# A two-block network on one core: the norms of the second block tile by tile, shifted copies on two engines, and the entries of the feed-forward stages reordered

## The chip, the core and the metric

The kernel runs on one core of one Trainium2 chip, as a single program of its five engines: TensorE (PE), VectorE (DVE), ScalarE (ACT), GpSimd (POOL) and SyncE (SP), which here issues all the DMAs. The metric is the time of the whole program on the device in microseconds (us). The profile's span runs from the first to the last instruction; the program's time is a little longer.

## The reference

Two blocks follow one another on a batch of one, 256 tokens (two tiles of 128), width 1024, all in float32.

```
h = x
for l in 0, 1:                                   # first block
    h = layer_norm(a*h + 0.5*swiglu(h, ffn1[l]))     # hidden width 2816
    h = layer_norm(a*h + mixer(h))                   # three branches: delta rule, conv, latent attention
    h = layer_norm(a*h + 0.5*swiglu(h, ffn2[l]))
# second block: four residual steps j = 0..3, each
#   shift, scale, gate = split(silu(c) @ mod_w[j] + mod_b[j])
#   x = x + gate * fn_j(rms_norm(x, g[j]) * (1 + scale) + shift)
# fn_0: short convolution (in 1024 -> 3072, 3 taps, out)   fn_1: swiglu
# fn_2: dilated attention                                 fn_3: router, top 2 of 8 experts, swiglu each
out = rms_norm(x, final_g)
```

## The kernel before, in words

Everything stays in SBUF: H holds the 256 rows as two tiles t = 0, 1 of [128, 1024]. Each engine has a program of its own in which the stages stand in a fixed, hand-written order; semaphores join them. There is no planner. Weights come by SP in tiles of 1 MB.

**Split products.** In the first block and in the FFNs each float32 operand is split into a high part (ScalarE's copy into the rounded format, semaphores ..._high) and a remainder (VectorE's subtraction, L1058 for weights, ..._low), and each product is three matmuls (L715, L716, L717).

**An FFN** (ffn_pe, ffn_act, ffn_vec) has NS = 11 steps of 256 hidden columns. TensorE does gate(0), up(0), gate(1), up(1), down(0), then in a loop gate(s), up(s), down(s-1), and last down for tile 0 and then for tile 1, so that the norm of tile 0 starts early. VectorE's step s is: remainder of gate(s+1); one part of the modulation (mod_vec, L1048 and L1051: eight operations that add mod_w rows into mod_sum, in four of the five FFNs); unit product silu(gate)*up; remainders of up(s+1) and down(s); remainder of the unit. Before it stands the split of the stage's input: turned_act (L935) and turned_vec (L1079) in the first block, x_high_act and x_low_vec (L1073) in the second. SP asks for the next weights when the remainder of the last ones is done (gate_load, up_load, down_load), in program order with mod_load.

**Norms of the first block.** layer_norm on VectorE: L1178 adds the residual (one operand in PSUM), L1181 and L1183 take the statistics, L1186 and L1190 subtract, scale and shift (two operands in SBUF each); std_act on ScalarE (L1028) takes the root between them. Then TensorE turns the tile (turn_h, L711). After the second FFN of a layer TensorE first sums mod_sum by mod_pe (L889: 24 blocks, two matmul records each), which ScalarE takes to mod_col (mod_act). spin (L883) is matmuls whose result is not used.

**Norms of the second block**, for j = 0..3: residual on VectorE (L2395, L2397) with the gate's row, rms_act on ScalarE (square L2246, root L2248, both tiles in turn), norm_vec (L2383) on VectorE, turns on TensorE (norm_pe), then norm_act: ScalarE makes eight scaled and shifted copies of 256 columns to HT (L2256), two for each of four PSUM banks ("quarters"), and after them two copies of the gate's row (L2265), which TensorE has made by four matmul records (L2075) from diag. TensorE waits for HT (ht_ready) and for the row (grow_ready) before it goes on to the stage: L2095 (convolution in), the FFN, L2127 (attention projections) or L2192 (router).

GpSimd has only the constants, one product per layer (L688) and five products per layer of 128x1024 (L695) in the mixer.

## Time and profile before

| what | value |
|---|---|
| time, median of 3 runs | 3021.76 us (3019.57 to 3026.18) |
| the profiled execution's own time | 3022.93 us |
| its span | 3021.2 us |
| mean granted clock of TensorE | 0.981 |
| TensorE busy | 2888.2 us, 96% |
| VectorE busy | 2016.1 us, 67% |
| ScalarE busy | 1440.2 us, 48% |
| GpSimd busy | 52.8 us, 2% |
| memory read | 657.23 MB, 218 GB/s over the span |
| chain that ended last | PE 76%, DVE 9%, PEld 4%, issue 3%, ACT 3% |
| one operation of L1051, mean | 484 ns |

The chain that ended last is followed back from the last instruction to whatever released each one. A granted clock of 1 is 2.4 GHz, 0.5 is 1.2 GHz. In a row of the timeline the first two numbers are start and duration in us, "x8" is the number of instructions merged in the row, and the square brackets tell how long the engine idled before it and whose instruction ended that. In a table of windows the busy time of PE, PEld, DVE, ACT and POOL follows the length.

### The profile page before, as it was taken

How to read it: one execution, taken by the hardware profiler on the slowest of the kernel's cores; microseconds unless marked ns; L12 is line 12 of the kernel's file. 1: busy time of each engine (PE TensorE's matmuls, PEld its weight loads, DVE VectorE, ACT ScalarE, POOL GpSimd, SP SyncE). 2: the span in 40 equal slices, each digit the busy share in tenths (PEclk: the TensorE clock that was granted, in tenths of full speed). 3: DMA queues.
4: the chain of work that ended last, by engine and by line, in shares of the span. 5: the costliest groups of instructions: out<-in, count | busy, mean ns of one | idle time of the engine just before them, and what ended most of it. 6: DMA issues, size and time to landing. Idle time of an engine off the chain costs nothing.

```text
span 3021.2 us, 43641 instructions
## 1 busy us (share of the span) xinstructions
PE 2888.2 (96%) x16718; PEld 2451.4 (81%) x16718; DVE 2016.1 (67%) x2457; ACT 1440.2 (48%) x1600; POOL 52.8 (2%) x93
## 2 busy tenths in 40 slices
PE   8999898999999998899999999988999999999997
PEld 8998886699899988758988699455888888888886
DVE  6767963477777787327651444154898889888987
ACT  4434621244444462114530344133777777777775
POOL 2000010000000001000000000000000000000000
PEclk9999999999999999999999999998999999999999
DMA  8755512486777442137743455323999999999995
GB/s 296 249 168 174 158 57 86 147 270 222 243 246 237 154 139 96 58 112 259 242 139 140 151 186 179 106 74 121 358 349 339 349 348 347 341 349 348 347 341 210
DMA packets 398878, 659.74 MB, mean 218 GB/s; under 512 B 14090, under 2 KB 241272, under 8 KB 398776
## 3 DMA queue, kind: packets, MB, share of 16 engines
q1 hardware_dynamic: 398776, 658.32, 63.1%
q8 instruction: 72, 1.18, 0.2%
q14 instruction: 30, 0.25, 0.0%
HBM read 657.23 MB, written 1.05 MB: 218 GB/s over the span
## 4 chain that ended last, share of the span: by engine, by line
PE 76%; DVE 9%; PEld 4%; issue 3%; ACT 3%; DVEq 2%; DMA 1%; PEldq 1%; ACTq 0%; SPq 0%
PE banks L715 20%; PE banks L716 19%; PE banks L717 19%; PE banks L2095 3%; PE banks L2127 3%; PE banks L1392 2%; PE banks L711 2%; DVE ffn_arena L1058 1%; PE banks L788 1%; DVE mod_sum L1051 1%; PE banks L889 1%; PEld banks L1392 1%; PE banks L883 1%; DVE panel_rest L1744 1%; PE banks L1362 1%
## 5 line engine op out<-in xcount | busy, mean ns | idle before, releaser
L715 PE MATMUL banks<-ffn_arena 128*128 128x256 f32 (+1 forms) x3460 | 1163.3, 336 | 23.3 <-DVE ffn_arena L1079 10.3
L717 PE MATMUL banks<-ffn_arena 128*128 128x256 f32 (+1 forms) x3460 | 1148.6, 332 | 0.0
L715 PEld LDWEIGHTS banks<-ffn_arena 128*128 128x128 f32 x3460 | 660.4, 191 | 93.8 <-DVE ffn_arena L1079 12.6
L717 PEld LDWEIGHTS banks<-ffn_arena 128*128 128x128 f32 x3460 | 660.3, 191 | 69.5
L1120 DVE TENSOR_TENSOR expert_rest<-expert_raw,ffn_arena 128x2048 fp32r<-128x2048 f32 (+1 forms) x306 | 646.8, 2159 | 83.9 <-ACT ffn_arena L977 79.4
L716 PE MATMUL banks<-ffn_arena 128*128 128x256 f32 (+1 forms) x2200 | 672.2, 306 | 0.0
L977 ACT ACTIVATE ffn_arena<-expert_raw 128x2048 fp32r<-128x2048 f32 (+1 forms) x306 | 539.4, 1815 | 66.9 <-PE banks L717 64.5
L716 PE MATMUL banks<-expert_rest,ffn_arena 128*128 128x512 f32 (+1 forms) x1224 | 465.8, 381 | 0.0
L716 PEld LDWEIGHTS banks<-ffn_arena 128*128 128x128 f32 x2200 | 422.9, 192 | 17.4 <-issue 0.5
L716 PEld LDWEIGHTS banks<-expert_rest,ffn_arena 128*128 128x128 f32 x1224 | 230.0, 188 | 42.8
L1058 DVE TENSOR_TENSOR ffn_arena<-gate_w,ffn_arena 128x1024 fp32r<-128x1024 f32 x110 | 130.0, 1223 | 195.5 <-ACT ffn_arena L912 195.5
L912 ACT ACTIVATE ffn_arena<-down_w 128x1024 fp32r<-128x1024 f32 x110 | 110.4, 1051 | 162.1 <-PE banks L717 149.4
L715 PE MATMUL banks<-ffn_arena,mix_high 128*128 128x256 f32 x640 | 181.9, 284 | 4.6 <-DVE panel_rest L1744 2.6
L717 PE MATMUL banks<-ffn_arena,panel_rest 128*128 128x256 f32 x640 | 180.0, 281 | 0.0
L716 PE MATMUL banks<-ffn_arena,mix_high 128*128 128x256 f32 x640 | 180.0, 281 | 0.0
L1051 DVE SCALAR_TENSOR_TENSOR mod_sum<-mod_unit,misc_col,mod_sum 128x256 f32 (+1 forms) x336 | 162.7, 484 | 25.1
L912 ACT ACTIVATE ffn_arena<-up_w 128x1024 fp32r<-128x1024 f32 x110 | 110.5, 1053 | 120.4 <-PE banks L717 111.6
L1058 DVE TENSOR_TENSOR ffn_arena<-down_w,ffn_arena 128x1024 fp32r<-128x1024 f32 x110 | 129.6, 1219 | 48.5 <-ACT ffn_arena L912 48.5
L912 ACT ACTIVATE ffn_arena<-gate_w 128x1024 fp32r<-128x1024 f32 x110 | 109.9, 1050 | 65.4 <-PEq L2110 59.9
L1542 ACT ACTIVATE arena<-banks 128x512 f32<-128x512 f32 (+3 forms) x100 | 55.2, 592 | 175.4 <-PE banks L1352 52.5
L1058 DVE TENSOR_TENSOR ffn_arena<-up_w,ffn_arena 128x1024 fp32r<-128x1024 f32 x110 | 129.6, 1219 | 4.7 <-ACT ffn_arena L912 4.7
L1744 DVE TENSOR_TENSOR panel_rest<-panel,mix_high 128x2048 fp32r<-128x2048 f32 x48 | 109.6, 2286 | 30.6 <-ACT mix_high L1542 30.2
(412 smaller groups left out, 3410.3 us busy)
## 6 DMA issues: line engine op xcount, KB each, us to landing
expert_raw<-in_moe_w_gate_dram SPq DMA_DIRECT2D x90, 1024.0 KB, 5.3
expert_raw<-in_moe_w_up_dram SPq DMA_DIRECT2D x90, 1024.0 KB, 5.4
expert_raw<-in_moe_w_down_dram SPq DMA_DIRECT2D x90, 1024.0 KB, 5.1
gate_w<-in_ffn_w_gate_dram SPq DMA_DIRECT2D x55, 1024.0 KB, 5.3
up_w<-in_ffn_w_up_dram SPq DMA_DIRECT2D x55, 1024.0 KB, 5.4
down_w<-in_ffn_w_down_dram SPq DMA_DIRECT2D x55, 1024.0 KB, 5.4
mod_unit<-in_mod_w_dram SPq DMA_DIRECT2D x48, 1024.0 KB, 5.2
panel<-in_w_in_dram SPq DMA_DIRECT2D x48, 1024.0 KB, 5.4
```

Of the source, the lines that this page charges most:

```text
L715: mm(out, w[0], x[0], start=start, stop=False)
L716: mm(out, w[0], x[1], start=False, stop=False)
L717: return mm(out, w[1], x[0], start=False, stop=stop)
L912: act_fn(weights[0][:, half, :], tile[:, half, :], ACT.Copy).then_inc(high, 1)
L977: act_fn(high[:, half, :], tile[:, half, :], ACT.Copy).then_inc(expert_hi, 1 if h else 1 + skipped)
L1051: stt(mod_sum[:, cols], mod_w[:, k, :], misc_col[:, k:k + 1], mod_sum[:, cols], ALU.mult, ALU.add)
L1058: last = tt(weights[1][:, half, :], tile[:, half, :], weights[0][:, half, :].bitcast(F32), ALU.subtract)
L1120: tt(rest[:, half, :], tile[:, half, :], high[:, half, :].bitcast(F32), ALU.subtract).then_inc(expert_lo, 1 if h else 1 + skipped)
L1392: last = mm(banks[:, 4 + j, half * SEQ:(half + 1) * SEQ], tile[:, k, b * P:(b + 1) * P], src[:, k, :], start=k == 0, stop=k == kb - 1)
L1744: tt(rest, raw_, high.bitcast(F32), ALU.subtract).then_inc(half_low, 1)
L2095: last = mm(banks[:, 4 + i % 4, half * SEQ:(half + 1) * SEQ], tile[:, k, c:c + P], HT[:, k, :], start=k == 0, stop=k == KD - 1)
L2127: last = mm(banks[:, 4 + i % 4, 0:cols], HT[:, k, t * P:(t + 1) * P], tile[:, k, :], start=k == 0, stop=k == KD - 1)
```

## The change

- rms_act, norm_vec and residual work tile by tile: residual_tile(0), norm_tile(0), then the same for tile 1; at j = 0 the squares wait for the last layer norm directly and stand ahead of mod_act. At j = 2 the normed tiles lie at another place of the arena.
- The shifted copies: ScalarE quarters 0 and 2, VectorE quarters 1 and 3. At j = 1 ScalarE writes the high half of the split straight from PSUM (norm_high_act) and VectorE writes HT.
- TensorE does not wait for the gate's row after the norm; its matmuls go to banks 2 and 3.
- Fewer spins: none instead of 4 at j = 0, 3 instead of 4 (and between the tiles) at j = 1 to 3, spin(2, 1) goes, spin(0, 2) becomes spin(0, 1).
- In the first block: the last norm product of tile 1 and the turn and split of tile 1 are halved by columns (norm_half, x_half). The remainder of the first gate tile of three FFNs (second FFN of either layer, first of layer 1) is GpSimd's, and ScalarE's copy for it moves ahead of the root of tile 1.
- Layer 1's first FFN: turns of tile 0 come first, then half of mod_pe, turns of tile 1, the other half.
- ffn_vec: step 0 is taken out of the loop, with mod_vec(1) behind the unit product and the remainder of up(1).
- norm_start(0) stands before the last layer norm.

```diff
             for l in range(DEPTH):                               # GpSimd, after the products of the mixer
+                for first in (l * FFN_LAYER + NS, l * FFN_LAYER + FFN_LAYER)[:2 if l + 1 < DEPTH else 1]:
+                    for i, half in enumerate((slice(0, KD // 2), slice(KD // 2, KD))):
+                        pool.wait_ge(gate_high, first * 2 + i + 1)
+                        last = nc.gpsimd.tensor_tensor(gate_parts[1][:, half, :], gate_w[:, half, :], gate_parts[0][:, half, :].bitcast(F32), ALU.subtract)
+                    last.then_inc(gate_low, 1)
...
-        def turn_h(pe, done, fill=0):
+        def turn_h(pe, done, fill=0, mod=None):
             for t in range(TT):
                 if t == 1 and fill:
                     spin(5, fill)
-                pe.wait_ge(norm_done, done + t + 1)
+                if t == 1 and mod is not None:
+                    mod_pe(pe, mod, banks[:, 0, 0:12], range(12))
+                if t == 0:
+                    pe.wait_ge(norm_done, done + 1)
                 for half in range(2):
+                    if t == 1 and half == 0:
+                        pe.wait_ge(norm_half, done // 2 + 1)
+                    elif t == 1:
+                        pe.wait_ge(norm_done, done + 2)
...
+            if mod is not None:
+                mod_pe(pe, mod, banks[:, 0, 12:24], range(12, 24)).then_inc(mod_col_done, 1)
...
         def turned_vec(dve, f):
+            dve.wait_ge(x_high, f * 2 + 1)
+            tt(x_parts[1][:, :, 0:P], turned_tile(0), x_parts[0][:, :, 0:P].bitcast(F32), ALU.subtract).then_inc(x_low, 1)
+            dve.wait_ge(x_half, f + 1)
+            tt(x_parts[1][:, 0:4, P:], turned_tile(1)[:, 0:4, :], x_parts[0][:, 0:4, P:].bitcast(F32), ALU.subtract)
+            dve.wait_ge(x_high, f * 2 + 2)
+            tt(x_parts[1][:, 4:8, P:], turned_tile(1)[:, 4:8, :], x_parts[0][:, 4:8, P:].bitcast(F32), ALU.subtract).then_inc(x_low, 1)
...
-            with dve.Fori(0, NS - 1) as s:
+            gate_vec(dve, n, 1)
+            unit_vec(dve, n, 0, FB * SEQ)
+            up_vec(dve, n, 1)
+            if m is not None:
+                mod_vec(dve, m, 1, slice(MOD_COLS, 2 * MOD_COLS))
+            down_vec(dve, n, 0)
+            dve.wait_ge(unit_high, n + 1)
+            tt(unit_parts[1], act_t, unit_parts[0].bitcast(F32), ALU.subtract).then_inc(act_ready, 1)
+            with dve.Fori(1, NS - 1) as s:
                 step(s)
...
+                    stt(H[:, t, 0:512], H[:, t, 0:512], spread[:, t, 1:2], row_b[:, 0:512], ALU.mult, ALU.add).then_inc(norm_half, 1)
+                    stt(H[:, t, 512:D], H[:, t, 512:D], spread[:, t, 1:2], row_b[:, 512:D], ALU.mult, ALU.add).then_inc(norm_done, 1)
...
             def norm_pe(j):
-                spin(5, (4, 4, 4, 4)[j])
                 for t in range(TT):
+                    if t == 1:
+                        spin(1, NORM_SPINS[j])                   # (0, 3, 3, 3)
...
-                    last = mm(banks[:, i, :], ones[:], diag[:, 4 * i:4 * i + 4, :].rearrange("p b c -> p (b c)"), start=True, stop=True)
+                    last = mm(banks[:, 2 + i, :], ones[:], diag[:, 4 * i:4 * i + 4, :].rearrange("p b c -> p (b c)"), start=True, stop=True)
                 last.then_inc(grow_done, 1)
-                pe.wait_ge(ht_ready, 4 * (DEPTH + 1 + j))
-                pe.wait_ge(grow_ready, j + 1)
+                if j != 1:
+                    pe.wait_ge(ht_ready, 4 * (DEPTH + 1 + j))
...
-                std_act(act, l * LN_LAYER + 2, LN_EPS)
+                std_act(act, l * LN_LAYER + 2, LN_EPS, [0])
                 gate_act(act, n + NS, 0)
+                std_act(act, l * LN_LAYER + 2, LN_EPS, [1])
...
+                std_act(act, l * LN_LAYER + 3, 4 * LN_EPS, [0])
+                if l + 1 < DEPTH:
+                    act.wait_ge(down_done, n + 2 * NS + 1)
+                    gate_act(act, n + FFN_LAYER, 0)
+                std_act(act, l * LN_LAYER + 3, 4 * LN_EPS, [1])
...
+            def norm_high_act(j):
+                for q in range(4):
+                    act.wait_ge(turned, 4 * (NORMS + j) + q + 1)
+                    if q == 2:
+                        act.wait_ge(ht_ready, 4 * (DEPTH + j) + 2)
+                    for half in range(2):
+                        b = 2 * q + half
+                        last = act_fn(x_parts[0][:, b, :], banks[:, 4 + q, half * SEQ:(half + 1) * SEQ], ACT.Identity,
+                                      scale=mod_scale[:, b:b + 1], bias=mod_col[:, 24 * j + b:24 * j + b + 1])
+                    if q % 2:
+                        last.then_inc(x_high, 1)
+                grow_act(j)
...
+            rms_act(0)
             norm_act(0)
+            mod_act(act, 2 * DEPTH - 1, banks[:, 0, 0:24])
...
+            rms_act(1, [0])
             act.wait_ge(mix_done, DEPTH + 1)
             gate_act(act, FFN2, 0)
-            norm_act(1, True)
+            rms_act(1, [1])
+            norm_high_act(1)
...
-            residual(0, acc, NORMS + 1, (mix_done, DEPTH + 1))
-            norm_vec(1)
+            residual_start(0)
+            dve.wait_ge(tile_done, NORMS + 1)
+            residual_tile(0, acc, 0)
+            norm_tile(1, 0)
+            dve.wait_ge(mix_done, DEPTH + 1)
+            residual_tile(0, acc, 1)
+            norm_tile(1, 1)
             gate_vec(dve, FFN2, 0)
+            norm_vec(1, (2, 3))
+            dve.wait_ge(x_high, (FFNS - 1) * 2 + 1)
+            norm_vec(1, (0, 1))
+            dve.drain()
             x_low_vec(dve, FFNS - 1)
```

The same order of residual_tile and norm_tile stands at j = 2 and 3, with norm_vec(j, (1, 3)) behind it: VectorE's four copies.

## Rows read from the trace of the kernel before

**Rows 1.** TensorE's waits, whole span: who waited for whom, us in total, times, longest.

```profile
PE banks L715 <- DVE ffn_arena L1079: 10.3, 4, 4.5
...
PE banks L715 <- DVE ffn_arena L1058: 5.2, 3, 1.8
PE banks L883 <- ACT row_g L2265: 4.8, 1, 4.8
```

**Rows 2.** Timeline, layer 0, mixer to second FFN: start, us, engine, line, operation, count.

```profile
576.39 1.28 DVE L1190 SCALAR_TENSOR_TENSOR H<-H,spread,row_b 128x1024 f32<-128x1024 f32 x1
...
578.87 1.22 DVE L1178 SCALAR_TENSOR_TENSOR H<-H,banks 128x1024 f32<-128x1024 f32 x1 [1.19 <-PEq L1531]
...
584.48 2.35 DVE L1058 TENSOR_TENSOR ffn_arena<-gate_w,ffn_arena 128x1024 fp32r<-128x1024 f32 x2
...
586.75 2.35 DVE L1079 TENSOR_TENSOR ffn_arena<-banks,ffn_arena 128x1024 fp32r<-128x1024 f32 x2
```

**Rows 3.** Timeline of GpSimd and VectorE in layer 0's mixer.

```profile
372.28 2.34 POOL L695 TENSOR_TENSOR arena<-arena,level 128x1024 f32<-128x1024 f32 x1 [78.66 <-DVEq L1883]
372.28 3.42 DVE L1885 TENSOR_TENSOR arena<-arena,level 128x1024 f32<-128x1024 f32 x1
375.78 1.23 DVE L1887 TENSOR_TENSOR arena<-ident,arena 128x1024 f32<-128x1024 f32 x1
```

**Rows 4.** Timeline, a later stretch of the same mixer.

```profile
425.80 2.36 POOL L695 TENSOR_TENSOR arena<-arena,level 128x1024 f32<-128x1024 f32 x1 [3.75 <-PE banks L1352]
...
427.54 0.69 DVE L1911 TENSOR_TENSOR arena<-arena,banks 128x512 f32<-128x512 f32 x1 [3.04 <-PE banks L1362]
```

**Rows 5.** Timeline, layer 0's last norm into layer 1's first FFN.

```profile
779.10 6.73 PE L889 MATMUL banks<-ones,mod_sum 128*128 128x1 f32 x48 [0.35 <-DVE H L1190]
...
783.36 1.28 DVE L1190 SCALAR_TENSOR_TENSOR H<-H,spread,row_b 128x1024 f32<-128x1024 f32 x1
...
785.69 3.65 PE L711 MATMUL banks<-ident,H 128*128 128x128 f32 x16
...
789.31 2.35 DVE L1079 TENSOR_TENSOR ffn_arena<-banks,ffn_arena 128x1024 fp32r<-128x1024 f32 x2
```

**Rows 6.** Windows: length, busy us (count) by engine, granted clock, DMA share, GB/s.

```profile
783.20:790.00 6.80, 6.14 (x29) 5.74 (x28) 4.34 (x6) 3.62 (x5) 0.00 (x0) 0.50 0.00 0
1558.00:1568.20 10.20, 10.20 (x32) 7.39 (x32) 7.27 (x22) 2.88 (x8) 0.00 (x0) 0.50 0.01 2
1575.35:1590.95 15.60, 15.59 (x64) 13.12 (x64) 0.00 (x0) 0.60 (x1) 0.00 (x0) 0.90 0.00 0
```

**Rows 7.** Timeline, entry of the second block.

```profile
1563.23 6.16 PE L883 MATMUL banks<-level,ident 128*128 128x512 f32 x8
...
1575.35 6.96 PE L2095 MATMUL banks<-HT,panel 128*128 128x256 f32 x24 [2.49 <-issue]
```

**Rows 8.** Timeline, norm 1 into the second block's FFN.

```profile
1707.63 1.52 PE L883 MATMUL banks<-level,ident 128*128 128x512 f32 x2 [4.80 <-ACT row_g L2265]
```

**Rows 9.** Timeline, norm 2 into the attention's projections.

```profile
1897.02 0.20 ACT L2248 ACTIVATE spread<-moments 128x1 f32<-128x1 f32 x1
...
1897.38 1.22 DVE L2395 TENSOR_TENSOR ffn_tmp<-banks,row_g 128x1024 f32<-128x1024 f32 x1 [2.92 <-PE banks L717]
...
1900.26 0.75 DVE L2383 TENSOR_SCALAR arena<-H,spread 128x1024 f32<-128x1024 f32 x1
...
1902.48 1.09 PE L711 MATMUL banks<-ident,arena 128*128 128x128 f32 x8 [0.31 <-DVE arena L2383]
1902.95 3.75 ACT L2256 ACTIVATE HT<-banks,mod_col,small 128x256 f32<-128x256 f32 x8 [1.56 <-PE banks L711]
...
1903.41 1.88 PE L2075 MATMUL banks<-mod_unit,ones 128*128 128x512 f32 x4
...
1907.78 4.53 PE L2127 MATMUL banks<-panel,HT 128*128 128x512 f32 x10 [2.49 <-issue]
```

**Rows 10.** Timeline, norm 3 into the router.

```profile
2075.54 5.81 PE L2192 MATMUL banks<-router,HT 128*128 128x8 f32 x32 [2.53 <-ACT row_g L2265]
```

More of the change, by code:

```diff
@@ L932, in turned_act @@
         def turned_act(act, before):
-            for t in range(TT):
-                act.wait_ge(turned, before + 2 * t + 2)
-                act_fn(x_parts[0][:, :, t * P:(t + 1) * P], turned_tile(t), ACT.Copy).then_inc(x_high, 1)
+            act.wait_ge(turned, before + 2)
+            act_fn(x_parts[0][:, :, 0:P], turned_tile(0), ACT.Copy).then_inc(x_high, 1)
+            for half, done in ((slice(0, 4), x_half), (slice(4, 8), x_high)):
+                act.wait_ge(turned, before + 2 + half.stop // 4)
+                act_fn(x_parts[0][:, half, P:], turned_tile(1)[:, half, :], ACT.Copy).then_inc(done, 1)
         def x_high_act(act, x=x_parts, width=SEQ):
@@ L2069, in norm_pe @@
                             b = 2 * q + half
-                            last = turn(banks[:, 4 + q, half * SEQ + t * P:half * SEQ + (t + 1) * P], x_norm[:, t, b * P:(b + 1) * P])
+                            last = turn(banks[:, 4 + q, half * SEQ + t * P:half * SEQ + (t + 1) * P], normed[j][:, t, b * P:(b + 1) * P])
                         if t == TT - 1:
@@ L2258, in norm_act @@
                     last.then_inc(ht_ready, 1)
[L2259 to L2266 removed]
+                grow_act(j)
[10 more added lines that the diff above has]
+                        last.then_inc(x_high, 1)
+                grow_act(j)
+            rms_act(0)
             norm_act(0)
+            mod_act(act, 2 * DEPTH - 1, banks[:, 0, 0:24])
             for i in range(8):
@@ L2633, in _ @@
             dve.drain()
-            residual(3, experts_sum)
+            residual_start(3)
+            for t in range(TT):
+                residual_tile(3, experts_sum, t)
             dve.wait_ge(norm_in, NORMS * 32 + 16)
```

152 lines of the change are left out of this document (89 added, 63 removed).

## The prediction

> **What bounds the kernel now.** TensorE is busy for 96% of the span, so time is to be had in two ways only: where TensorE waits, and where it works at the lower of its two clocks. I read the page for the shares, then TensorE's waits, then the timeline at every seam between two matmul stages. Inside a feed-forward (FFN) TensorE never waits except near its start: three waits on VectorE's L1058 sum to 5.2 us, the four FFNs of the first block wait 10.3 us in all for their split input (L1079), and the second block's FFN waits 4.8 us for ScalarE's copy of the gate's row [rows 1]. The change touches only seams. Expert work after the router starts from the route's result, so it moves as a whole with it.
>
> **The second step of an FFN (gain 5.2).** VectorE now does the unit product and up_vec(1) ahead of mod_vec(1), in the step that was peeled from the loop. mod_vec stood ahead of the remainder of the up weights that TensorE waited for, in three of four FFNs, 1.8 us at the longest and 5.2 us in all [rows 1]. It is eight operations over 256 columns, about half a microsecond each, so some 4 us: more than the longest wait, and the waits go whole. Late next: down_vec(0) and its unit remainder, which by my walk through the step come some 0.8 us ahead of TensorE's need; the second mod load is asked for later by about the same 4 us less the wait, and up(2) and down(1) behind it on SP's queue; up(2) still lands some 2 us ahead of its use, as a step of TensorE is longer than one of VectorE. In the first FFN nothing waits there, so nothing is gained.
>
> **Entry of the second FFN of a layer, twice (gain 1.3 each).** Now VectorE's last norm product is followed by the split of the gate weights, 2.35 us, and that of the input, 2.35 us, after which TensorE starts at 589.1 [rows 2]. The change gives the gate's split to GpSimd, and puts ScalarE's copy for it between the two tiles' roots, so at about 575. What that collides with is a row: VectorE's L1885, two operands in SBUF, took 3.42 us while GpSimd's L695 took 2.34, and L1887, of the same size, took 1.23 alone [rows 3]. So VectorE stood still for 2.2 us, the whole of GpSimd's instruction. An operation with one operand in PSUM was not held: L1911 took 0.69 inside a GpSimd operation of 2.36 us [rows 4]. I price a GpSimd half at 2.35 us, from those rows; it is 128x1024 here too. First half: from 576.2 to 578.6. L1190 of tile 0 is due at 576.39 [rows 2], now 578.6 to 579.9. Second half: to 582.2, over L1178 (PSUM, not held), which starts at 579.8 instead of 578.87, 0.9 us late. All that follows is 0.9 us late, to the end of the last norm product, 585.45. Then the input's split without the gate's before it: 1.13 + 0.6 + 0.6 us, in halves, to 587.8. Against 589.1 that is 1.3 us. One instruction more on each engine by the halving (about 0.1 us each) is in it. If GpSimd runs both halves without letting VectorE in, L1178 starts at 582.2, TensorE at 590.2: a loss of 1.1. If nothing is held, 586.9: a gain of 2.2. I take alternation, since VectorE asks first.
> The Trainium skill ("SBUF — State Buffer", Who interferes with whom) says the same of the pair: the engine that issues first has the shared ports for its whole instruction, against VectorE operations with two SBUF inputs, and the other is blocked fully. By it the statistics (one input) would run under GpSimd, which I assume and no row shows. The rule speaks against this move, and the trace agrees with it; the sum by it is the one above, where "GpSimd costs VectorE nothing" would have given 0.9 us more at each.
>
> **Layer 1's first FFN (loss 1.5).** Before, the 48 modulation records (6.73 us) stand ahead of the 16 turns, 3.65 us at the lower clock; the input's splits end at 791.66 [rows 5]. Now tile 0's turns and half of the records run while VectorE norms tile 1. GpSimd's halves start when the last down product ends plus one ScalarE copy, 779.9. VectorE's L1186 is held to 782.2, then GpSimd again to 785.85, and L1190, due at 783.36 [rows 5], starts 2.5 us late. Turns from 786.6, eight at 0.23 us (3.65/16) to 788.4, then 24 records: 3.4 us at 6.73/48 each, 5.5 us at 0.23. TensorE starts the FFN at 791.8 to 793.9 against 791.66. The clock was 0.50 from 783.2 to 790 [rows 6], and I expect much of it again: 793.2, a loss of 1.5. Bounds: 2.7 us better if nothing holds VectorE, 2.3 worse if the clock stays low into the FFN.
>
> **Entry of the second block (gain 6.3).** Square and root of both tiles no longer queue behind mod_act, whose input ends at 1563.2, and four spins (eight records, 6.16 us) go [rows 7]. The normed tiles are ready at 1563.4, as the modulation ends. Then 16 turns at 0.23 are 3.7 us, and four records of the gate's row 3.1 us (half of 6.16): first product at 1570.0. The shifted copies are by then done, since they are divided. Before: 1575.35, so 5.3 us. That stretch then ran at 0.90 of the clock for 15.6 us [rows 6], 1.6 us lost behind 2.49 us of idling; with no idling I expect to keep 1.0. Bounds of the term 4.0 and 7.
>
> **Norm 1, to the FFN (gain 1.3).** The FFN starts after the spin at 1707.63 + 1.52 = 1709.15 [rows 8]. Now tile 0 is squared under the convolution's last products. ScalarE writes the high half from PSUM while VectorE makes the shifted copy. Walk: tile 1's turns 0.6 us earlier; VectorE: gate split 2.35 to 1701.5, four copies (0.3 to 0.5 us each, a fourth of L1058's 1.2 as the low end, ScalarE's 3.75/8 [rows 9] as the high one; 0.43 taken) to 1703.2, four more to 1705.0, two splits of 1.2 each, 1707.3. That is 1.85, less 0.5, as the FFN's first products take the spin's place at the lower clock.
>
> **Norm 2 (gain 1.6).** The first tile's root comes from ScalarE at 1897.22, and tile 1's residual started at 1897.38 [rows 9]. The tile's norm now stands between (0.75 and small ones), so residual, root and turn of tile 1 are 0.8 us late: the turn at 1903.3 for 1902.48. But from the turn to the first product it was 5.3 us, eight copies in 3.75, then the row's copies; now copies in two engines take 1.9, and the row's four records, which follow 0.9 us after the turn's start and take 1.88, are the end: 2.9 us. 5.3 - 2.9 - 0.8 = 1.6.
>
> **Norm 3 (gain 3.4).** Here tile 1 is far behind tile 0 and nothing is late: 2.4 us by the same count. The router's 32 records took 5.81 [rows 10]; at 6.73/48 each [rows 5] they would take 4.5. Of this, and of the spins after, I count 1.0 (0 to 3.3).
>
> **Nothing.** The halved turn of the first FFN costs 0.1. Halved norms before the mixer are covered by the products of tile 0 (about 5 us; uncovered 0.1). norm_start(0) is 2.1 us in a VectorE wait of 3.2 ahead of the last norm. The order of mod_col and the output semaphore's count move no work. The final norm is unchanged.
>
> **Sum.** 5.2 + 2.6 - 1.5 + 6.3 + 1.3 + 1.6 + 3.4 - 0.1 = 18.8 us, from the profiled execution's own 3022.93 (span 3021.2 and 1.7 around it): 3004.1. The median shown is 1.2 below that execution: 3003.
>
> **Rivals.** (1) GpSimd's two halves run back to back: 2.4 us worse at each of the two entries, 0.3 at layer 1: 13.7 gained, 3008. For it: both halves are waiting by then; against: VectorE asks first. (2) GpSimd holds nothing, since the rows of a hold are of other operations: 1.8 and 2.7 better, 23.3 gained, 2998.5. Against: [rows 3] is plain. (3) The clock: fewer spins and more small products leave the lower clock standing where it did not. A stretch of 6.8 us [rows 6] at half speed costs 3.4; two or three more of these leave 9 to 12 gained, 3011. (4) Slower: a GpSimd half that rounds to the split format takes far longer than the 2.34 of plain float32. Each us adds two at each of three entries, so at 2.34 + 18.8/6 = 5.5 us all is eaten, and beyond it the kernel is slower; at 4 us the time is 3013, at 7 us 3031. No row has that format on GpSimd. (5) Most does not carry: the seams are replaced by new waits of the same length (down(0) late by 0.8 us of slack, up(2) behind the mod load), 3 to 8 gained, 3016.
>
> **How the numbers follow.** Forecast 50% (3000 to 3006), rival 1 20%, 2 12%, 3 9%, 4 4%, 5 5%. The range 2997 to 3012 holds the forecast, 1, 2 and most of 3. A difference under 0.2% (6 us) is what a measurement cannot tell from none. Faster 0.92, same 0.04, slower 0.04.
>
> **What would show it.** Waits of TensorE on L1058 near each FFN's second up gone; GpSimd halves near 2.35 us, with VectorE's norm products at 3.4 or more beside them; entries 1.3 us shorter; the first conv product about 5 us earlier behind the last norm; no wait on ScalarE's row copy. It is wrong if GpSimd's halves are longer, if both run before VectorE gets in, or if the granted clock falls in stretches where it stood at 2.4 GHz.

## The result, and the profile after

| | before | after |
|---|---|---|
| time, median (lowest to highest) | 3021.41 us (3019.57 to 3026.18, 4 runs) | 2994.48 us (2992.94 to 2996.65, 4 runs) |
| ratio, 95% interval | | 0.9905 (0.9891 to 0.9920) |
| the profiled execution's own time | 3022.93 us | 2996.65 us |
| its span, mean granted clock | 3021.2 us, 0.981 | 2994.9 us, 0.984 |

The gain is 26.9 us by the medians, 26.3 by the two spans and 28.7 by the ratio (24 to 33 by its interval); 18.8 was forecast, and 2994.5 lies below the range of 2997 to 3012. The sign and most seams came as said; the size did not.

TensorE's waits of the changed kernel, whole span (who waited for whom, us in total, times, longest), beside [rows 1]:

```profile
PE banks L725 <- DVE ffn_arena L1094: 10.6, 2, 5.5
...
PE banks L725 <- DVE ffn_arena L1102: 6.0, 3, 4.4
PE banks L721 <- DVE arena L2449: 5.6, 5, 1.7
PE banks L721 <- DVE H L1224: 4.5, 3, 3.4
```

L1094 is the input's split of the second block and L1102 that of the first (L1079 in the code before). No matmul waits for the up weights' remainder any more, and none for the gate's row: both rows of before are gone. L1224, the halved norm product, is new, 3.4 us of it at one place.

Timeline, mixer to second FFN of layer 0, beside [rows 2]:

```profile
574.24 5.65 POOL L705 TENSOR_TENSOR ffn_arena<-gate_w,ffn_arena 128x1024 fp32r<-128x1024 f32 x2 [148.04 <-ACT ffn_arena L931]
574.26 0.16 DVE L1219 RECIPROCAL spread<-spread 128x1 f32<-128x1 f32 x1
574.49 3.18 DVE L1222 SCALAR_TENSOR_TENSOR H<-H,spread,row_b 128x1024 f32<-128x1024 f32 x1
577.59 1.21 DVE L1209 SCALAR_TENSOR_TENSOR H<-H,banks 128x1024 f32<-128x1024 f32 x1
578.87 1.29 DVE L1212 BATCH_NORM_STATS2 stats<-H 128x6 f32<-128x512 f32 x2
...
585.05 0.68 DVE L1102 TENSOR_TENSOR ffn_arena<-banks,ffn_arena 128x512 fp32r<-128x512 f32 x1
```

This is the lock that the prediction priced. GpSimd starts first, VectorE's product with two operands in SBUF takes 3.18 us instead of 1.28, and it gets in before GpSimd's second half. The first half takes 2.35 us, the second, which waits for VectorE's product, 3.34, and both together 5.65, not 4.7. The residual with an operand in PSUM (1.21) and the statistics (1.29) run under the second half at their usual length. The FFN starts 8.87 us after the mixer's last product for 10.34.

Timeline, layer 1's first FFN, beside [rows 5]:

```profile
774.68 5.63 POOL L705 TENSOR_TENSOR ffn_arena<-gate_w,ffn_arena 128x1024 fp32r<-128x1024 f32 x2 [194.79 <-ACT ffn_arena L931]
774.80 2.74 PE L899 MATMUL banks<-ones,mod_sum 128*128 128x1 f32 x24
...
778.26 2.60 DVE L1224 SCALAR_TENSOR_TENSOR H<-H,spread,row_b 128x512 f32<-128x512 f32 x1
...
780.91 1.97 PE L721 MATMUL banks<-ident,H 128*128 128x128 f32 x8 [3.38 <-DVE H L1224]
...
782.68 5.12 PE L899 MATMUL banks<-ones,mod_sum 128*128 128x1 f32 x24
```

Here GpSimd's second half runs ahead of VectorE's half product, which takes 2.60 us for 0.75; it is the only operation held for long. TensorE waits 3.38, and the second 24 records take 5.12 us for the 2.74 of the first: 1.2 GHz against 2.4.

Timeline, entry of the second block, beside [rows 7]:

```profile
1544.76 6.48 PE L899 MATMUL banks<-ones,mod_sum 128*128 128x1 f32 x48 [0.37 <-DVE H L1222]
1551.62 3.68 PE L721 MATMUL banks<-ident,arena 128*128 128x128 f32 x16 [0.38 <-DVE arena L2449]
...
1555.09 2.30 PE L2112 MATMUL banks<-mod_unit,ones 128*128 128x512 f32 x4
...
1557.22 2.97 PE L2132 MATMUL banks<-HT,panel 128*128 128x256 f32 x13
```

Norm 2 into the attention's projections and the router's product, beside [rows 9] and [rows 10]:

```profile
1884.55 1.09 PE L721 MATMUL banks<-ident,arena 128*128 128x128 f32 x8 [1.65 <-DVE arena L2449]
1885.03 1.94 ACT L2307 ACTIVATE HT<-banks,mod_col,small 128x256 f32<-128x256 f32 x4 [1.94 <-PE banks L721]
1885.25 1.90 DVE L2456 TENSOR_SCALAR HT<-banks,small,mod_col 128x256 f32<-128x256 f32 x4 [0.75 <-PE banks L721]
1885.48 1.88 PE L2112 MATMUL banks<-mod_unit,ones 128*128 128x512 f32 x4
1887.20 1.98 PE L2164 MATMUL banks<-panel,HT 128*128 128x512 f32 x4
...
2051.03 4.08 PE L2229 MATMUL banks<-router,HT 128*128 128x8 f32 x32
```

The copies run in two engines at once, the row's four records end last, and from the turn to the projections it is 2.65 us (2.9 forecast). At the second block's entry the convolution starts 12.83 us after the FFN instead of 20.35, and in the convolution's first 15.6 us the clock is at 2.4 GHz throughout (third window below, for 0.90 in [rows 6]). Windows of the changed kernel (length, busy us of PE, PEld, DVE, ACT, POOL, granted clock, DMA share, GB/s): the start of a second FFN, layer 1's first seam, the convolution, the start of the second block's FFN.

```profile
585.80:596.00 10.20, 10.20 (x85) 10.20 (x86) 7.17 (x12) 4.61 (x5) 0.00 (x0) 1.00 0.57 182
777.70:791.40 13.70, 10.48 (x50) 10.49 (x51) 8.59 (x10) 3.35 (x6) 2.61 (x1) 0.50 0.26 77
...
1557.30:1572.90 15.60, 15.49 (x72) 13.33 (x71) 0.95 (x5) 2.36 (x5) 2.46 (x8) 1.00 0.03 4
1688.00:1694.00 6.00, 6.00 (x34) 6.00 (x35) 2.22 (x2) 0.58 (x1) 0.00 (x0) 0.63 0.43 125
```

**Where the 26.3 us came from.** Measured is the length of each stage, from first matmul to first matmul, in the two profiled spans. "Half clock" is 1.2 GHz.

| part | forecast | measured |
|---|---|---|
| peel: the three FFNs where TensorE waited | 5.2 | 1.9 + 0.2 + 3.6 = 5.7 |
| entries of the second FFNs | 2 x 1.3 | 2 x 1.47 |
| layer 1's first FFN | -1.5 | -1.2 |
| entry of the second block | 6.3 | 7.5, and 1.6 inside the convolution |
| norm 1 | 1.3 | 0.4 at the seam, -1.1 in the FFN |
| norm 2 | 1.6 | 1.5 |
| norm 3 | 3.4 | 2.7 at the seam, 1.7 in the router's product, 0.1, and 1.3 ahead of it in the attention's last stages |
| first FFN | -0.1 | 1.2 |
| first products of either mixer | 0 | 2 x 1.6 |
| inside the mixers | 0 | -0.9, -0.4 |

Summed over the clock's records, the kernel before runs 114.9 us at 1.2 GHz and the changed one 94.1. Half of the difference, 10.4 us, is what the clock gives at most (where TensorE waits anyway, it gives nothing). Without it 15.9 us are left; the forecast without its two clock terms of 1.0 was 16.8.

Two entries of the table can't be credited to the edits, as later_start (the kernel before, started some 2 us later) shows them too. Its attention takes 154.5 us, where the kernel before took 157.3 and the changed one 156.0; so the 1.3 us ahead of norm 3 can't be told from chance. Its convolution takes 117.4 us, like the changed kernel's 117.3, for 118.9 before. All thirteen versions with the second block's edits have the short convolution, but so do two of the four without them, and the 1.6 us are at best in part an effect of the change.

### The profile page after: what moved, and what is told of

Read it like the earlier page. It is cut to its first block, busy times and chain, and to the rows that moved or that the text cites. A ratio compares the mean times of both kernels' runs of the same rounds, so it can differ in the third digit from the quotient of the medians.

```text
span 2994.9 us, 43574 instructions
## 1 busy us (share of the span) xinstructions
PE 2869.0 (96%) x16698; PEld 2441.5 (82%) x16698; DVE 2026.5 (68%) x2481; ACT 1434.2 (48%) x1590; POOL 69.0 (2%) x99
## 4 chain that ended last, share of the span: by engine, by line
PE 82%; DVE 9%; ACT 2%; issue 2%; DVEq 2%; DMA 1%; PEld 1%; PEldq 1%; ACTq 0%; SPq 0%
PE banks L725 21%; PE banks L726 21%; PE banks L727 21%; PE banks L1427 3%; PE banks L2132 3%; PE banks L2164 3%; PE banks L721 2%; PE banks L1562 1%; PE banks L798 1%; PE banks L1268 1%; DVE ffn_arena L1079 1%; PE banks L899 1%; PE banks L1397 1%; PE banks L1503 1%; PE banks L1387 1%
## 5 line engine op out<-in xcount | busy, mean ns | idle before, releaser
L1079 DVE TENSOR_TENSOR ffn_arena<-gate_w,ffn_arena 128x1024 fp32r<-128x1024 f32 x104 | 122.9, 1223 | 181.2 <-ACT ffn_arena L931 181.1
L1079 DVE TENSOR_TENSOR ffn_arena<-down_w,ffn_arena 128x1024 fp32r<-128x1024 f32 x110 | 129.6, 1220 | 48.1 <-ACT ffn_arena L931 47.6
L1079 DVE TENSOR_TENSOR ffn_arena<-up_w,ffn_arena 128x1024 fp32r<-128x1024 f32 x110 | 129.8, 1221 | 10.7 <-ACT ffn_arena L931 10.7
L725 PEld LDWEIGHTS banks<-ffn_arena,mix_high 128*128 128x128 f32 x640 | 121.5, 190 | 6.5 <-issue 3.5
```

What stands on the lines that cost most here:

```text
L725: mm(out, w[0], x[0], start=start, stop=False)
L1079: last = tt(weights[1][:, half, :], tile[:, half, :], weights[0][:, half, :].bitcast(F32), ALU.subtract)
```

## The experiments

Times are medians with lowest, highest and number of runs; the ratio is to the kernel before on the same chip. The kernel before had a median of 3022.0 us over 53 executions. Each execution also reports its mean granted clock; its average is the last column.

| run | time, us | ratio (95%) | clock |
|---|---|---|---|
| before | 3022.0 (3016.31 to 3029.31, 53) | | 0.9818 |
| later_start | 3022.76 (3018.53 to 3029.51, 11) | 1.0004 (0.9995 to 1.0013) | 0.9822 |
| peel_alone | 3018.27 (3014.71 to 3025.31, 11) | 0.9987 (0.9977 to 0.9997) | 0.9807 |
| first_block_alone | 3008.76 (3006.82 to 3017.41, 7) | 0.9961 (0.9948 to 0.9974) | 0.9823 |
| second_block_alone | 3009.26 (3007.57 to 3010.50, 5) | 0.9956 (0.9942 to 0.9969) | 0.9814 |
| after | 2994.48 (2992.94 to 2996.65, 4) | 0.9905 (0.9891 to 0.9920) | 0.9847 |
| after_again | 2995.03 (2993.81 to 2996.01, 4) | 0.9907 (0.9892 to 0.9923) | 0.9845 |
| after_later | 2997.81 (2994.79 to 2999.78, 5) | 0.9915 (0.9901 to 0.9929) | 0.9838 |
| no_peel | 3001.64 (3000.82 to 3003.31, 5) | 0.9929 (0.9916 to 0.9943) | 0.9842 |
| gate_on_vector | 3001.87 (3000.26 to 3006.66, 5) | 0.9938 (0.9924 to 0.9952) | 0.9818 |
| gate_spun | 3001.45 (2997.89 to 3003.16, 5) | 0.9929 (0.9915 to 0.9942) | 0.9822 |
| norm1_gpsimd | 2997.29 (2996.78 to 3003.25, 5) | 0.9920 (0.9906 to 0.9935) | 0.9830 |
| norm1_filled | 2996.03 (2993.75 to 2999.76, 5) | 0.9907 (0.9893 to 0.9921) | 0.9830 |
| norm1_scalar | 2997.27 (2992.11 to 2999.83, 6) | 0.9912 (0.9898 to 0.9926) | 0.9827 |
| better | 2993.65 (2991.58 to 2995.67, 4) | 0.9901 (0.9886 to 0.9917) | 0.9840 |
| filled | 2993.09 (2990.99 to 3000.02, 4) | 0.9899 (0.9883 to 0.9914) | 0.9838 |
| mended_filled | 2996.79 (2991.66 to 2997.44, 5) | 0.9908 (0.9894 to 0.9923) | 0.9830 |

**The parts.** peel_alone is the kernel before with the new ffn_vec; first_block_alone and second_block_alone split all edits in two; no_peel is the changed kernel with the old ffn_vec:

```diff
-            gate_vec(dve, n, 1)
-            unit_vec(dve, n, 0, FB * SEQ)
...
-            with dve.Fori(1, NS - 1) as s:
+            with dve.Fori(0, NS - 1) as s:
```

> The kernel before with the new ffn_vec alone (step 0 outside the loop, the second modulation part behind the remainder of up(1)). Forecast: the three waits of 5.2 us go and nothing else, 3016. Theory 'phase': the waits go and the low stretches after them move too, 5 to 10 us in all. Rival: the later mod load delays up(2) and a wait comes back, under 3 us gained.

> The kernel before with the second block's part of the change alone: norms tile by tile, early squares, divided copies, no wait for the gate's row, fewer spins. The first block is as before. Forecast: 6.3 + 1.3 + 1.6 + 3.4 = 12.6 us gained, 3009. By the trace of the changed kernel (9.1 at the entry with the convolution's products, 0.7 lost at the FFN, 1.5, 1.2 in the attention, 4.3 to the experts): 15.5, 3006. More than 18 or less than 9 would say that the clock's share depends on the first block's timing.

> The kernel before with the first block's edits alone; norms, spins and copies of the second block stay as before. Theory A, waits removed and nothing else: 5.2 + 2 x 1.3 - 1.5 - 0.1 = 6.2 us, 3015.5. Theory B, each removed wait of TensorE also removes time at 1.2 GHz behind it: what the second block's edits alone left of the whole gain (27 less 12 to 13) is all here, 13 to 15 us, 3007 to 3008, and the third FFN from the front of layer 1's pair, 190.97 us before, takes 187.4 to 187.8. Between 8 and 12 the two parts are not independent.

> The changed kernel with the FFN's step 0 back inside the loop, the modulation's part ahead of the unit product and the up remainder. Theory A, the peel is worth the three waits it removes, which are 1.8 us each: 5.2 us slower, 2999.7, the waits back. Theory B, alone on the kernel before the peel gave 3 to 4 us, because the clock took 1.8 back in one FFN: 2997 to 2998.5. If the waits bring the clock down as well, it is above 3001.

The second block's part is 0.44%, 13.3 us (9 to 18 by the interval), where 12.6 were forecast: right. The first block's part is 0.39%, 11.8 us (8 to 16), for 6.2: here lies the excess. By the ranges set down above this is short of theory B (13 to 15) and still in the range that was to mean that the parts are not independent, though layer 1's second FFN takes the 187.6 us that theory B gave it. Its profile is 16.1 us shorter than that of before, and 6.4 of these lie in the attention (2.8) and inside the mixers (3.6), where nothing was edited. Together the parts make 25 of the 28 to 29 us that the changed kernel's ratios give, so they nearly add. The peel shows where a part of the excess comes from. Waits of TensorE on VectorE's weight remainders in no_peel, whole span, and the half-clock window behind the one in layer 1's second FFN, beside the same place in the changed kernel:

```profile
PE banks L725 <- DVE ffn_arena L1079: 7.5, 4, 2.4
...
1383.47 0.39 PE L725 MATMUL banks<-ffn_arena 128*128 128x256 f32 x1 [1.98 <-DVE ffn_arena L1079]
...
1385.00:1388.40 3.40, 3.40 (x18) 3.40 (x17) 3.40 (x4) 0.61 (x1) 0.00 (x0) 0.50 1.00 349
```

```profile
1378.00:1381.40 3.40, 3.40 (x26) 3.18 (x25) 3.40 (x4) 0.42 (x1) 0.00 (x0) 1.00 1.00 332
```

TensorE waits 1.98 us, and 1.5 us later the clock is at 1.2 GHz for 3.4 us: 18 matmuls for 26. The kernel before has the same pair, a wait of 1.74 at 1383.3 and the clock at 0.50 from 1383.9. In the profiles of four kernels with this wait the stretch is there four times (before, later_start, second_block_alone, no_peel); without the wait it is there in none of twelve, gate_on_vector left out, whose low stretch lies at that FFN's start. It is not a rule for every wait: the one of 1.6 to 1.8 us in layer 0's second FFN is followed by such a stretch in one of the four (second_block_alone, from 608.5) and by none in the others. The waits come to 7.5 us here, 5.1 in the three FFNs and 2.4 in the first, where the kernel before has none (why stays open). In ratio no_peel is 0.22 to 0.24%, 7 us, behind the changed kernel, for the 5.2 forecast; the intervals overlap a little, the single executions do not. These 7 us are no more than the waits themselves: that the half-clock stretch costs the whole program time besides is not shown by this run. On the kernel before, the peel gave only 3.9 (1 to 7 by the interval); its clock is the lowest of all kernels (0.9807).

**GpSimd's remainder.** gate_on_vector takes GpSimd's loop out and puts gate_vec back in front of turned_vec; gate_spun also puts spins in the longer wait:

```diff
-                    last.then_inc(gate_low, 1)
...
+                gate_vec(dve, n + NS, 0)
                 turned_vec(dve, l * 2 + 1)
...
-                spin(0, 1)
+                spin(0, 4)
```

> The changed kernel with the gate's remainder back on VectorE at the three entries (ScalarE's copy stays early). By the lock: each second FFN's entry loses 2.35 and regains 0.9, so 1.4 later twice; at layer 1 VectorE is no longer held, the turns come 2.2 us earlier and the gate's remainder is behind the modulation's matmuls: 2 us gained. Sum 0 to 1 us slower. Rival (GpSimd's help is worth its whole 2.35 at each): 5 to 7 us slower.

> The changed kernel with GpSimd's halves of the gate remainder back on VectorE, as in the run before this one that measured 3001.87 us, and four spins instead of one ahead of the second FFN of each layer. The spins fill the 3.08 us in which TensorE waited for the split there and leave nothing to delay it by (3.1 us at 2.4 GHz). Theory A, the clock is what the longer wait costs: both second FFNs begin at 2.4 GHz, the 5.8 and 6.1 us of them that ran at 1.2 GHz go, and the time is 2996.5 (5.3 less). Theory B, the half-clock stretches in those FFNs have nothing to do with the wait and fall by chance of phase: 3001 to 3002.5, with stretches as before them.

At the seams gate_on_vector did what the sum said: both second FFNs start 1.67 us later, layer 1's first 1.97 earlier. Yet it is 0.33% (10 us, 7.4 by the medians) slower, where 0 to 1 us was expected. First matmul of the FFN and the window behind it, gate_on_vector and then gate_spun:

```profile
587.41 0.58 PE L719 MATMUL banks<-ffn_arena 128*128 128x256 f32 x1 [3.08 <-DVE ffn_arena L1096]
...
587.40:596.00 8.60, 8.59 (x50) 8.59 (x51) 5.88 (x10) 0.00 (x0) 0.00 (x0) 0.66 0.75 244
```

```profile
583.97 3.60 PE L887 MATMUL banks<-level,ident 128*128 128x512 f32 x8
588.07 0.39 PE L719 MATMUL banks<-ffn_arena 128*128 128x256 f32 x1 [0.51 <-DVE ffn_arena L1096]
...
588.10:596.00 7.90, 7.90 (x66) 7.90 (x67) 5.84 (x10) 1.80 (x3) 0.00 (x0) 1.00 0.79 244
```

Where TensorE is idle for 3.08 us, the FFN starts at 1.2 GHz (5.8 us of it, and 6.1 in layer 1, where 0 were before); with the wait filled it starts at 2.4, as long after the mixer (10.54 us), and the two FFNs take 187.5 and 187.7 us for 190.2 each. Nothing else differs, so in these profiles the wait is the cause of those stretches. But of these 5.2 us, which were expected in the time (2996.5), 2.7 show in the ratios and 0.4 in the medians, not separable from none: in gate_spun the entry of the second block has 10.2 us at half clock instead of 6.8, and the mean clock of its executions is hardly higher (0.9822 for 0.9818).

**Chance of the place in time.** later_start and after_later are the kernel before and the changed one with two VectorE memsets ahead of the first turns, so that everything starts some 2 us later; after_again is the changed kernel once more.

```diff
+            for i in range(2):
+                nc.vector.memset(arena[:, 8192 + 1024 * i:9216 + 1024 * i], 0.0)
```

> The kernel before, with two memsets of 128x1024 on VectorE ahead of the first conversion, so that all that follows starts some 1.5 to 2.5 us later. Nothing else differs. Theory 'seams' (the clock follows the program's own work, so its low stretches move with it): slower by those 1.5 to 2.5 us and no more, 0.05 to 0.08%, the low stretches at the same places of the work. Theory 'phase' (where the low stretches fall depends on when the work meets the clock's own beat, and part of the 26.9 us is that): a change of another size, anywhere from 8 us faster to 6 us slower, with low stretches at the starts of the FFNs and mixers that are there in one kernel and not in the other.

> The changed kernel with its first 16 turns some 1.7 us later behind two added VectorE operations at the start, nothing else changed. Theory A, the missing half-clock stretches of the changed kernel come from shorter idling at the seams: their sum stays at 82 to 88 us and the time at 2994 to 2997. Theory B, they come from where the seams fall in time: the sum moves back towards the 106 us of the kernel before, at least in the mixers' entries (5.2 us for 32 records instead of 3.7), and the time is 2998 to 3004.

> The changed kernel once more. If the 94 us at half clock in its first profile belong to it, this profile shows 90 to 98 and the time is 2993 to 2996.5; if they were a lucky phase, it shows more than 100, or the ratio to the kernel before rises to 0.992 or more.

later_start runs the same seams, and its profile has other low stretches: none at the mixers' first products, where the kernel before has these two, but 27.3 us for 17.1 in the first mixer.

```profile
209.70:213.10 3.40, 3.40 (x18) 3.40 (x19) 2.64 (x3) 0.58 (x4) 0.00 (x0) 0.50 0.00 0
...
984.60:988.00 3.40, 3.40 (x18) 3.40 (x17) 2.33 (x3) 0.57 (x4) 0.00 (x0) 0.50 0.01 2
```

So the 3.2 us that the table above shows at the mixers' first products can't be called an effect of an edit: later_start has neither stretch without any, and after_again has the first of them (208.9 to 212.3) with all. The changed kernel's high clock did come again (91.1 us at half clock, 0.9845), and its later twin keeps most of it (94.8 us, 0.9838), at a time 0.1% higher that the intervals do not separate. The expectation of after_later counts without the stretch at the very end of the span; so counted it has 85.3 us, as the changed kernel does, for 105.8 before, as its theory A said.

**Norm 1.** The copies back on ScalarE; the gate's remainder on GpSimd; three spins in TensorE's wait:

```diff
-            norm_vec(1, (2, 3))
-            dve.wait_ge(x_high, (FFNS - 1) * 2 + 1)
-            norm_vec(1, (0, 1))
-            dve.drain()
```

```diff
-            gate_vec(dve, FFN2, 0)
```

```diff
             norm_pe(1)
+            spin(1, 3)
```

> The changed kernel with norm 1's copies back on ScalarE alone, eight copies and two high halves as before the change; VectorE has only the gate's remainder and the two splits there. By the prediction's term the division was worth 1.85 us of a later start of the FFN: 2996.3. Theory B, VectorE's chain in the changed kernel (2.36, 3.70, 2.36) is as long as ScalarE's was (1.93, 1.06, 1.91, 1.06, and a last split of 1.22 behind it): the FFN starts within 0.6 us of the changed kernel's, 2994.5 to 2995.

> The changed kernel with the remainder of the second block's first gate tile given to GpSimd. Theory A, norm 1 gained nothing because VectorE's own chain there (2.36 us of gate remainder, eight copies of 0.46, two splits in 2.36) is as long as the one that it took from ScalarE: without the first term the eight copies begin with the turns, 1.6 to 1.8 us earlier, GpSimd's halves holding at most the norm's product; 2992.7 to 2993. Theory B, TensorE's wait there was for something else (the up weights, ScalarE): no change, 2994.5; or GpSimd's halves hold the norm products of both tiles and it is 0 to 1 us slower.

> The changed kernel with three spins behind the row's product of norm 1, inside the wait of 5.53 us that TensorE has there. They issue in 2.3 us at 2.4 GHz or 4.6 at 1.2, and end before the wait does. Theory A, the wait is what sends the clock down: the FFN starts at the same time with matmuls at 2.4 GHz, takes 187.3 to 188 us instead of 190.26, and the time is 2992 to 2993. Theory B, the clock is set by something else (the sparse work before the norm, or chance): the 6.8 us at half clock stay, the FFN takes 189 to 190.3, 2994.5.

Timeline of the changed kernel, then of norm1_scalar:

```profile
1679.52 2.36 DVE L1079 TENSOR_TENSOR ffn_arena<-gate_w,ffn_arena 128x1024 fp32r<-128x1024 f32 x2
...
1681.79 3.70 DVE L2456 TENSOR_SCALAR HT<-banks,small,mod_col 128x256 f32<-128x256 f32 x8
...
1685.59 2.36 DVE L1094 TENSOR_TENSOR ffn_arena<-HT,ffn_arena 128x1024 fp32r<-128x1024 f32 x2
...
1688.00 0.58 PE L725 MATMUL banks<-ffn_arena 128*128 128x256 f32 x1 [5.53 <-DVE ffn_arena L1094]
```

```profile
1680.50 1.93 ACT L2317 ACTIVATE HT<-banks,mod_col,small 128x256 f32<-128x256 f32 x4 [1.56 <-PE banks L721]
...
1682.51 1.06 ACT L2323 ACTIVATE ffn_arena<-HT 128x1024 fp32r<-128x1024 f32 x1
1683.47 1.92 ACT L2317 ACTIVATE HT<-banks,mod_col,small 128x256 f32<-128x256 f32 x4
...
1685.47 1.06 ACT L2323 ACTIVATE ffn_arena<-HT 128x1024 fp32r<-128x1024 f32 x1
...
1686.56 1.23 DVE L1094 TENSOR_TENSOR ffn_arena<-HT,ffn_arena 128x1024 fp32r<-128x1024 f32 x1 [1.73 <-ACT ffn_arena L2323]
```

VectorE's three groups stand back to back, 8.4 us; with ScalarE alone the FFN starts 12.96 us after the convolution's last product instead of 13.49. The division of the copies costs 0.5 us at this seam, too little to show in the time (0.9912). Taking the remainder off VectorE did not help either (norm1_gpsimd, theory A fell). Timeline:

```profile
1678.33 5.63 POOL L717 TENSOR_TENSOR ffn_arena<-gate_w,ffn_arena 128x1024 fp32r<-128x1024 f32 x2 [113.59 <-ACT ffn_arena L935]
1678.48 3.28 DVE L2472 TENSOR_TENSOR H<-H,ffn_tmp 128x1024 f32<-128x1024 f32 x1
...
1683.52 1.00 DVE L2453 TENSOR_SCALAR arena<-H,spread 128x1024 f32<-128x1024 f32 x1
```

The residual's second step, two operands in SBUF, takes 3.28 us for 1.22 and all of tile 1 is late: the FFN starts 1.47 us later. In norm1_filled the FFN starts at the same 13.49 us, with 2.95 us of the wait left, and its first matmuls take 0.28 for 0.41. But 1.2 us later the clock falls all the same:

```profile
1693.70:1694.90 1.20, 1.18 (x10) 1.19 (x11) 1.20 (x2) 0.59 (x1) 0.00 (x0) 1.00 0.00 0
1694.90:1698.30 3.40, 3.40 (x19) 3.40 (x18) 1.03 (x1) 0.00 (x0) 0.00 (x0) 0.50 0.27 59
```

So 3.4 us of this FFN run at half clock for 4.5 in the changed kernel. The FFN is 1.5 us shorter (188.78 for 190.26); the larger part of that is a wait of 1.01 us on the unit's remainder near its end, which this profile does not have. The time is not shorter: 2996.0, and the profile has 108.4 us at half clock in all, for 94.1, with more in the first FFN (6.8 for 0), layer 1's mixer (27.3 for 20.5) and the attention (13.7 for 6.8).

**What the runs point to.** better gives the gate's remainder back to VectorE at layer 1's first FFN, behind the input's split, and lets VectorE do the first half of it at the second FFNs, in its wait between the tiles. filled adds norm1_gpsimd, the spins of norm 1 and two spins before the turns of tile 1 at layer 1's first FFN; mended_filled adds to better the spins of norm 1 alone.

```diff
+                    if gate is not None:
+                        dve.wait_ge(gate_high, gate * 2 + 1)
+                        half = slice(0, KD // 2)
+                        tt(gate_parts[1][:, half, :], gate_w[:, half, :], gate_parts[0][:, half, :].bitcast(F32), ALU.subtract).then_inc(angle_ready, 1)
                     dve.wait_ge(*whole)
```

> The changed kernel with two seams mended. Layer 1's first FFN: the gate remainder is VectorE's again, behind the input's split, so that GpSimd holds nothing there (2.0 us, as the run with it on VectorE showed). The second FFNs: VectorE does the first half of the gate remainder itself while it waits between the tiles (1.2 us in a wait of that length), GpSimd only the second. Theory A, the hold of the shared port is what those seams still pay: 1.0 us at each second FFN and 2.0 at layer 1, 2990.5 (4 less than the changed kernel). Theory B, VectorE's own half is as long as GpSimd's hold was, so only layer 1's 2.0 is won: 2992.5. If TensorE's idle time grows at either, the clock takes 2.5 us at each: 2995 or above.

> All that the runs point to: the kernel with the two seams mended (0.9901 of before), GpSimd's remainder at norm 1, and spins where TensorE waits: three ahead of the second block's FFN (wait of 3.9 us left, 2.3 us of spins at 2.4 GHz) and two before the second tile's turns at layer 1's first FFN (wait of 1.4 us). Theory A, filled waits keep the clock: 1.7 us from norm 1 and 1 to 2.5 us each from the clock at the two places, 2989 to 2991. Theory B, the clock does not follow the filling: 2992, as the spins then cost as much as they give. If spins run at 1.2 GHz they take 1.5 us each and delay the turns: 2994 or more.

> The two mended seams (2993.65, 0.9901 of before) with the three spins of norm 1 and VectorE's remainder there. Theory A, they add: 1.5 to 2.5 us from the clock in the second block's FFN, 0.9894 to 0.9896 of before, 2990.5 to 2992. Theory B, nothing from the spins: 0.990, 2993.5.

The seams of better moved as expected, if by less at the second FFNs: 8.27 us at both for 8.87 (1.0 was expected at each), 12.18 for 14.15 at layer 1, 3.2 us in all. Its time is 0.04% under the changed kernel's in ratio, which the intervals do not separate; nor do filled and mended_filled stand apart from it. The fastest profiled span is mended_filled's, 2989.9 us, but its median is 2996.8. At norm 1 mended_filled repeats norm1_filled, 3.4 us at half clock from 1.1 us into the FFN; filled has none in that FFN (187.3 us), which there starts 15.25 us after the convolution.

## Why the prediction was wrong

**The step that failed: the clock's share of the gain.** I counted 1.0 at the entry of the second block and 1.0 at norm 3, and nothing elsewhere. Measured are 5 to 10 us. The upper figure is the profile's (20.8 us less at half clock, halved). The lower one compares equal clocks: seven executions of the kernel before reported 0.984, with a mean span of 3016.4; three of the changed kernel and its repeat reported it too, 2994.2. That is 22.2 us without a difference in clock, of 26.9. (With three of the later twin, whose own start is some 2 us later, it is 20.9.) Of the 8.1 us over the forecast the clock is so 3 to 8. The seams besides are 1.7 over their terms in sum, 1.2 of it at the second block's entry; by the lower figure another 3 to 4 stay open. I took low stretches from the profile only where the change touched a seam, and treated the others as given, the one at 1383.9 inside an FFN among them, which stands right behind a wait that the peel removes. And rival 3 put the clock on the losing side alone, though nothing in the profile said so; the range ended at 2997 for that reason.

**How far the cause goes.** Shown by a change of the spins alone: the 3.08 us wait ahead of the second FFNs causes the half clock at their start, at both places (gate_spun). At norm 1 the same filling, with 2.95 us of the wait left, only kept the first 1.2 us at 2.4 GHz.

Shown by the versions side by side: norm 3. From the router's first product to the experts' first one, the four profiles without the second block's edits take 21.2 to 21.5 us, 10.2 of them at half clock. Of the thirteen with the edits, second_block_alone among them, twelve take 17.9, 3.4 at half clock; only the changed kernel's own profile has 6.8, and 19.6 us. Before and in after_again:

```profile
2075.50:2096.70 21.20, 21.16 (x70) 13.09 (x70) 8.14 (x48) 8.60 (x6) 0.00 (x0) 0.76 0.32 112
```

```profile
2051.10:2069.10 18.00, 18.00 (x72) 10.32 (x71) 10.08 (x57) 9.77 (x8) 0.00 (x0) 0.91 0.46 144
```

So the clock is worth 3.3 us here, where I counted 1.0, and the table's 1.7 is low. Which of the edits does it, the wait of 2.5 us on the row's copy that went or the spins, was not separated.

Seen together each time: the 1.7 to 2.0 us wait in layer 1's second FFN and its stretch; four profiles with a wait and a stretch, twelve with neither. Not the second block's edits: the 6.8 us at half clock at its entry for 10.2 before, since second_block_alone has 10.2 and first_block_alone 6.8; and gate_spun and filled have 10.2 again. Open: the total. Six other versions of the changed kernel (better, filled, mended_filled and the three of norm 1) average 0.9832 over 29 executions, none of the six above 0.984, and filling waits did not raise it. Against the changed kernel's 0.9846 that is up to 4 us of the 26.9 which may be a good place in time rather than the edits; what sets the low stretches inside the mixers, 34 to 48 us in every profile, was not tried.

**The peel: right, and in the profile worth a little more** (5.7 for 5.2). Its three waits went. What I named as late next, step 0's unit remainder, shows no wait. The wait on that line (L1128, 1.7 us over three places) stands some 180 us into an FFN, near its end; the kernel before has it too (L1105), 0.5 us over two.

**Second FFNs: right** (1.47 for 1.3), by alternation, not by rival 1 (back to back) or 2 (no hold). **Layer 1's first FFN: right** (1.2 for 1.5), though VectorE was held at one operation, not at two. **Second block's entry: right in its order** (7.5 for 6.3). With the second block's edits alone it is 6.2; the other 1.3 come with the 3.4 us less at half clock that first_block_alone has as well. Four records of the row took 2.30 us, where I took 3.1 at 1.2 GHz. For the 1.0 that I counted in the convolution see above: at best in part an effect of the change. **Norm 2: right** (1.5 for 1.6). **Norm 3: low** in the clock: its seam gave 2.7 for 2.4, and behind it the router's 32 records took 4.08 for 5.81, where I counted 1.0 of clock (3.3 in most versions).

**Norm 1: wrong, and small.** I forecast 1.3 and it lost 0.7. Lines of the kernel before:

```profile
1706.55 1.22 DVE L1073 TENSOR_TENSOR ffn_arena<-HT,ffn_arena 128x1024 fp32r<-128x1024 f32 x1 [1.73 <-ACT ffn_arena L2262]
...
1708.17 1.20 PE L715 MATMUL banks<-ffn_arena 128*128 128x256 f32 x1
...
1709.16 0.42 PE L716 MATMUL banks<-ffn_arena 128*128 128x256 f32 x1
```

The wait on the row's copy [rows 8] hid that the split of the input ended just as late, at 1707.77, 13.51 us after the convolution's last product. I set the end of VectorE's new chain at 1707.3 with copies at 0.43; they took 0.46, and the chain ended after 13.44 us, no earlier in effect than before. What went is the row's wait and the spin: the first matmul of before took 1.20 us, as the spin ahead of it was at work until about 1709.15 [rows 8]; counted to the second matmul the seam is 13.87 us for 14.90, 1.0 gained (0.4 when counted to the first, as in the table). The FFN behind it then lost 1.1, counted from its first matmul: 4.5 us at half clock for 3.4, and 1.01 us of waiting on the unit's remainder.

**Rival 4** (a half of 5.5 us or more on GpSimd) is out: 5.65 us is two halves (2.35 alone) with VectorE's operation between them.

**The lock.** The price of the alternation came from [rows 3]. The Trainium skill ("SBUF — State Buffer", Who interferes with whom) says that a VectorE instruction with two SBUF inputs contends with a GpSimd instruction that reads SBUF, and that one with at most one SBUF input, outside the performance modes that use two ports, does not. The trace agrees: 3.18, 2.60 and 3.28 us for VectorE's operations with two SBUF inputs under GpSimd, and no effect on the statistics with one (1.29).

## What to carry to other kernels

A wait removed from TensorE is worth its length and, at some places, the half-clock stretch behind it (half of its 3.4 or 6.8 us): look in the profile for low stretches right behind the waits that go, and put what is uncertain about the clock on both sides of the range. One profile can't tell a clock effect from a place in time: the same code started 2 us later had other low stretches, so compare the mean clock of many executions, and the same stage in the profiles of several versions, with the edit and without. Before an engine takes over half of another's chain, add up its own queue at that seam; at norm 1 the receiver was as long as the giver.

## What the runs showed of the hardware

- The total at half clock is not the sum of seams that one can mend one by one. Three versions with a filled wait began the stage behind it at 2.4 GHz (two of them, at norm 1, for 1.1 and 1.2 us only), and none has a mean clock that stands clear above that of the version without (0.9822 to 0.9818, 0.9830 to 0.9846, 0.9830 to 0.9840).
- Executions of one kernel differ together with their clock: the kernel before reported 0.978 to 0.984 over 53, and the mean span falls from 3025.0 at 0.980 (eight executions) to 3016.4 at 0.984 (seven).
- GpSimd's subtraction into the split format (2.35 us a half) holds VectorE as its plain product (2.34) did in [rows 3], and when both engines wait, they take turns: 2.35, VectorE's product, 3.34. An operation with one SBUF input was once stretched too, 1.00 us for 0.75, at GpSimd's end.
